# Two-block decoder on one core: rounding the next weights before the gates' sigmoid, and one split moved behind the second pooled product

## What is computed

```python
proj = rmsnorm(x, norm_mix_g) @ w_in
q, k, v, f_logit, cx, cb, cc, px, gate_logit = split(proj)
y_attn = forgetting_attention(q, k, v, logf) @ w_attn_out
y_conv = (cb * conv3(cc * cx)) @ w_conv_out
y_pool = pooling_mixer(px, pool_w, pool_scale)       # four small products, scaled by column
g = sigmoid(gate_logit)                              # three gates of width 1024
merged = g[0] * y_attn + g[1] * y_conv + g[2] * y_pool
x = x + merged @ w_o
x = x + (silu(gt) * up) @ w_ffn_out                  # gt, up = rmsnorm(x) @ w_ffn_in
```

## Time and profile before

| | us |
|---|---|
| median of 3 runs | 3363.87 (3363.17 to 3366.28) |
| the profiled execution | 3358.75 |
| its span, first to last instruction | 3356.6 |
| PE busy | 3220.8 (96%) |
| DVE busy | 1618.3 (48%) |
| ACT busy | 1085.7 (32%) |
| POOL busy | 322.1 (10%) |

### The profile page before, as it was taken

One profiled execution on the slowest core, in us unless ns is written; L12 is line 12 of the kernel. 1 busy time (PEld: TensorE's weight loads), 2 busy tenths in 40 slices (PEclk: granted clock), 3 DMA queues, 4 the chain that ended last, 5 costly groups with the idle time before them and its releaser, 6 DMA issues.

```text
span 3356.6 us, 38850 instructions
## 1 busy us (share of the span) xinstructions
PE 3220.8 (96%) x15546; PEld 2652.5 (79%) x15546; DVE 1618.3 (48%) x1917; ACT 1085.7 (32%) x1157; POOL 322.1 (10%) x178
## 2 busy tenths in 40 slices
PE   6986899999999899999999999999999999999999
PEld 5865698888888789888888777888888777888887
DVE  5365454555334644555534755444433674454433
ACT  2223233444322333444423332233322332233232
POOL 1003110011000001001100200101100120011000
PEclk9998899999999999999999999999999999999999
DMA  3410131222332123122233212222232212222223
GB/s 138 127 46 30 38 144 45 88 99 88 113 126 76 51 74 128 38 98 90 100 112 91 81 63 88 88 101 93 95 106 103 77 63 88 88 88 100 100 100 113
DMA packets 47578, 299.94 MB, mean 89 GB/s; under 512 B 7075, under 2 KB 7331, under 8 KB 13012
## 3 DMA queue, kind: packets, MB, share of 16 engines
q1 hardware_dynamic: 42336, 288.01, 24.3%
q10 hardware_dynamic: 5108, 10.02, 1.3%
HBM read 293.26 MB, written 4.75 MB: 89 GB/s over the span
## 4 chain that ended last, share of the span: by engine, by line
PE 90%; DVE 5%; ACT 2%; issue 1%; POOL 1%; DMA 0%; another core or an unknown queue 0%; ACTq 0%; DVEq 0%; SPq 0%; POOLq 0%
PE G L409 80%; PE psS L869 1%; PE G L876 1%; PE psS L681 1%; DVE wL L1342 1%; PE psT L901 1%; PE psT L490 1%; ACT wH L982 1%; PE psS L465 1%; PE psS L768 1%; PE G L775 1%; DVE mxt L1532 1%; PE psS L462 0%; DMA x<-in_x 0%; DVE ws L1814 0%
## 5 line engine op out<-in xcount | busy, mean ns | idle before, releaser
L409 PE MATMUL G<-hH,wH 128*128 128x512 f32 x2624 | 1042.3, 397 | 11.0 <-DVE wL L1342 5.9
L409 PE MATMUL G<-hH,wL 128*128 128x512 f32 x2624 | 1027.5, 392 | 2.1 <-issue 2.1
L409 PE MATMUL G<-hL,wH 128*128 128x512 f32 x2624 | 1027.7, 392 | 0.0
L1342 DVE TENSOR_TENSOR wL<-raw,wH 128x2048 fp32r<-128x2048 f32 x266 | 647.7, 2435 | 673.3 <-ACT wH L982 673.0
L409 PE MATMUL G<-wsr,wH 128*128 128x512 f32 (+1 forms) x2400 | 713.9, 381 | 14.3 <-DVE ws L2031 9.7
L982 ACT ACTIVATE wH<-raw 128x2048 fp32r<-128x2048 f32 x266 | 506.8, 1905 | 456.0 <-PE G L409 441.5
L409 PEld LDWEIGHTS G<-hH,wH 128*128 128x128 f32 x2624 | 497.6, 190 | 121.0 <-issue 16.4
L409 PEld LDWEIGHTS G<-hH,wL 128*128 128x128 f32 x2624 | 496.3, 189 | 108.3 <-issue 2.5
L409 PEld LDWEIGHTS G<-hL,wH 128*128 128x128 f32 x2624 | 496.7, 189 | 103.4 <-issue 2.4
L409 PEld LDWEIGHTS G<-wsr,wH 128*128 128x128 f32 x2400 | 445.4, 190 | 101.3 <-DVE ws L2031 10.6
L409 PE MATMUL G<-wsr,wL 128*128 128x512 f32 (+1 forms) x1200 | 456.2, 380 | 0.0
(11 more groups left out here) (259 smaller groups left out, 2769.6 us busy)
## 6 DMA issues: line engine op xcount, KB each, us to landing
raw<-in_units SPq DMA_DIRECT2D x266, 1024.0 KB, 4.8
ws<-bias_rows SPq DMA_DIRECT2D x2, 1536.0 KB, 14.8
bias_rows<-ws ACTq DMA_DIRECT2D x1, 2560.0 KB
x<-in_x SPq DMA_DIRECT2D x4, 512.0 KB, 8.2
ws<-in_mem ACTq DMA_DIRECT2D x2, 1024.0 KB, 4.9
ws<-bias_rows ACTq DMA_DIRECT2D x1, 2048.0 KB, 8.4
out_x<-x SPq DMA_DIRECT2D x4, 512.0 KB, 7.6
ws<-in_decay ACTq DMA_DIRECT2D x1, 1280.0 KB, 13.0
```

Source lines behind the costliest of these rows:

```text
L409: mm = pe.matmul(o, mv if swap else wt, wt if swap else mv, start=first and n == 0, stop=last and n == 2)
L1342: V.tensor_tensor(wL[:, g.p, :], raw[:, g.p, :], wH[:, g.p, :].bitcast(F32), ALU.subtract)\
```

## The change

On ACT the sigmoid leaves the reader and stands behind the whole `step`, so that the rounding of unit u+2 comes first and the sigmoid second; this holds for all ten units that `gates` handles in a layer. On DVE the split that followed the scaling of position 13 is taken away there and stands behind the second of the four pooled products.

```diff
@@ ACT, gates @@
                 def gates(first=0):
                     for jj in range(first, 4):
-                        def read(_):
-
-                            act.wait_ge(job_free, c.job.v + 3)
-                            store(ws[:, GATE + 2 * jj:GATE + 2 * jj + 2, :], ACT.Sigmoid)(
-                                ws[:, GATE + 2 * jj:GATE + 2 * jj + 2, :])
-                        step(read)
+                        step()
+
+                        act.wait_ge(job_free, c.job.v + 2)
+                        store(ws[:, GATE + 2 * jj:GATE + 2 * jj + 2, :], ACT.Sigmoid)(
+                            ws[:, GATE + 2 * jj:GATE + 2 * jj + 2, :])
@@ DVE, gates @@
-                        step(scaled(ws[:, GATE + 2 * jj:GATE + 2 * jj + 2, :]))
+                        step(scaled(ws[:, GATE + 2 * jj:GATE + 2 * jj + 2, :]), unit=first == 0 or jj == 2)
@@ DVE, pooled products @@
-                    step(pools, unit=jj == 3)
+                    step(pools, unit=jj in (1, 3))
```

## The result

| | before | changed |
|---|---|---|
| first measurement, median | 3363.52 us (4 executions, 3358.33 to 3366.28) | 3338.66 us (4, 3335.66 to 3351.54) |
| its ratio, 95% interval | | 0.9935, 0.9907 to 0.9964 |
| measured again, ratio | | 0.9954, 0.9937 to 0.9970 |
| a third time, ratio | | 0.9951, 0.9935 to 0.9968 |
| median (mean): before, the 75 executions run later; changed, all 23 | 3357.2 us (3357.5) | 3339.1 us (3341.1) |

The change is faster, by half a percent. The two repetitions, with 44 and 21 executions, give by their ratios 15.4 and 16.4 us, against 15.1 forecast, with intervals from 10 to 22 us; but the first median, 3338.66 us, lies 10 us under the forecast 3348.8 and outside of its range. The first two medians are 24.9 us apart, though the interval of their ratio, 12 to 31 us, holds the forecast difference.

What follows compares the result with a forecast made beforehand. PE was taken as the bound, with 90% of the time; only its waits and low clock could be won. Two layers at 3.7 + 3.85 us made 15.1 us, from 3363.87 to 3348.8 us; range 3344 to 3355.

Steps and rivals of the forecast that it cites:

- both places: Positions 14 and 19 in each layer of the second block: 3.7 and 3.85 us won per layer.
- the new wait: PE would stand still 2.2 us ahead of position 15, for the third pair of pooled readers, once per layer.
- DVE's wait for the rounding: In the gates, DVE's wait for ACT's rounding would fall from 2.9 us to under 1.
- What else moves costs nothing: At the other eight gate units of a layer the rounding comes about 2.2 us earlier, beside PE's matmuls, without cost.
- The cost of a fall: After the 2.2 us wait ahead of position 15 the clock drops, giving back 1.7 us per layer.
- I carry it to the median: 3363.87 - 15.1 = 3348.8 us: Whole program: the gain worked out on the profiled execution, 3358.75 us, was subtracted from the median, 5.1 us higher.
- for the scatter of the runs (3363.17 to 3366.28): Whole program: 1.5 us added on the low side of the range, which became 3344 to 3355 us.
- over 2 us falls and 1.2 us doesn't: PE's waits: clock fell to 0.54 and 0.55 after 2.07 and 2.23 us, stayed at 1.00 after 1.23.
- The rival of a clock that stays up: Position 15's new wait passes without a clock fall: 18.5 us won, 3345.4 us; chance 0.14.
- One place paying alone: Only one of positions 14 and 19 gains: about 7.5 us won, 3356.4 us; chance 0.10.
- time given back: PE is earlier but later waits for a resource that doesn't move, such as weight loads: 3364 us; chance 0.05.
- a clock that stays down: Clock falls when position 15 begins and stays low through positions 15 and 16: slower, 3384 us; chance 0.03.

Runs made afterwards that it cites:

- the second profile of before: A further profile of the kernel before, no edit; measured again that kernel had a median of 3356.8 us (33 executions), ratio 1.0002 against itself.
- ACT's half alone: Only the rounding ahead of the sigmoid on ACT, DVE's split left in place, against the kernel before: ratio 0.9959, 13.8 us faster.
- GpSimd's subtraction: GpSimd instead of DVE makes wL of position 15, an edit of the changed kernel: ratios to the kernel before 0.9941 and 0.9942, medians 3334.8 and 3337.0 us.

## Why the prediction was right and where it was wrong

**Right: both places, step by step.** At position 14 the order of events is the forecast one, and the stretch 8.26 against 8.2 us; the new wait, forecast at 2.2 us, is 1.86, since PE was through with the pooled jobs 6.4 us after the start of position 14 instead of 6.0, and DVE's third pair of readers, which ends the wait, came nearly when forecast. At position 19 it is 11.35 against 11.1 us, and DVE's wait for the rounding ahead of it is 0.87 us, forecast under 1. "What else moves costs nothing" is shown for the gates by the kernel with the rounding first at the last units only. The cost of a fall, 1.7 us forecast, is 7 matmuls in 10 us, 1.6 us.

**Right in sum, for the profile on which it was made, and there with some luck.** From the start of position 14 to that of position 24 the changed kernel needs 7.26 and 6.95 us less than that profile, 14.2 us against 15.1 forecast. Against the second profile of before it is 4.98 and 4.80, together 9.8 us, mostly because the clock did not fall at position 19 there: that it had fallen there twice in the profile that the sum used was luck. The executions give 15.4 and 16.4 us with intervals from 10 to 22, which hold the 14.2. What they have beyond the stretches would have to be falls elsewhere; no profile shows the change to cause that.

**Wrong, and the step that failed: "I carry it to the median: 3363.87 - 15.1 = 3348.8 us", and with it the 1.5 us that the range allowed "for the scatter of the runs (3363.17 to 3366.28)".** Three executions within 3 us looked like a kernel that repeats to 0.1%. By their times they were three of the lower clock, since no execution of the higher took more than 3359.1 us: 75 executions spread from 3348.4 to 3370.2, with a median of 3357.2. The base was 6.7 us too high. 3357.2 - 15.1 is 3342.1, already under the range. The median of the changed kernel's 23 executions lies another 3 us lower, at 3339.1; the two medians are 18.1 us apart, the means within the higher clock 15.8, and one cause is that 21 of 75 executions had the lower clock before and 3 of 23 behind the change. Whether the change makes the lower clock rarer cannot be told from three. The profiled execution, 3358.75 us and 5.1 us below the median of the three, was the hint; the prediction named that distance and did not ask where it came from. With 5.1 us more on its low side the range would have held 3339.1, though not yet the first median, 3338.66.

**Too sure: the fall of the clock as a matter of the wait's length.** The prediction read the earlier trace rows as a rule, over 2 us falls and 1.2 us doesn't. Over all twelve profiles the clock fell, during one of these waits or within 1.5 us behind it, in 9 of 12 cases at 1.85 to 1.88 us (8 of 10 ahead of position 15, 1 of 2 ahead of the fourth pooled job), in 4 of 8 at 2.23 to 2.25 us (2 of 6 at position 19, 2 of 2 where position 15 waited for its weights), in 2 of 2 at 2.76 us, in 4 of 4 at 4.87 and 4.88 us, and in none of 4 at 0.60 to 0.66 us. So position 19 was worth 3.6 us a layer against the profile that the prediction used and 2.1 against the other of before. The rival of a clock that stays up is not an alternative for the whole program, as the prediction had it, but a matter of each execution. The Trainium skill ("TensorE: Matmul & The Clock Gate", "HAM oscillation") blames only longer idle gaps; the falls behind 1.86 us speak against that for this kernel, as did the rows of before.

**The other rivals.** One place paying alone, time given back and a clock that stays down are all excluded by the stretches: both places pay in every profile of the changed kernel, the low clock behind position 15 is over after 10 us, and what follows is not longer than before: from the start of position 24 to the start of the layer's last product the first layer takes 306.5 us in the first profile of either kernel, and from the second layer's position 24 to the end both take 434.4.

**Open.** Why executions gather in two groups of clock, some 10 us apart, was not tried; the profiles show only that they part in the first block. Open too is what decides whether a wait of about 2 us costs clock in a given execution.

## What to carry to other kernels

When an engine's in-order queue holds work for a later consumer (here a split for the next unit) ahead of work that frees a buffer for the present one, put the latter first; count then what DVE must have done before PE's next start, since below that sum the order no longer matters and only another engine helps. What each half of a change is worth is read over a stretch that holds the fall of the clock of either: here ACT's half alone brought nearly everything, though its position 14 was 2 us longer. Before adding a gain to a base, ask how far the base itself moves: here an effect of some 15 us stood on executions that spread over 22 us, and only ratios against many executions on the same chip gave it. Where a profile and the median of its own program differ, that difference is the least width of a range.

## What the runs showed of the hardware

The granted clock fell to 0.50 (1.2 GHz) behind waits of PE as short as 1.85 us, in 9 of 12 cases, but not in all executions of the same program at the same place. It fell also in two stretches of the attention in which PE was busy throughout (50.00 us, 0.97 against 1.00 above), both times behind 16 matmuls of two columns that took 1.84 us together. A fall behind a wait of about 2 us cost about 1.6 us of matmuls (37 instead of 44 in 10 us). GpSimd's subtraction of 128x2048 took 4.6 us, as the profile times it, beside DVE's pooled readers, whose mean duration did not change by more than 2 ns (745 to 747 ns).
